# Where ScalarE computes the scan's turns, where GpSimd computes its fractions, and where the new-token bias products stand: one decoder layer step on one Trainium2 core

## The chip, the cores and the metric

The kernel runs on one core of one Trainium2 chip. The metric is the device time of one execution in microseconds (us); lower is better. TensorE is called PE here, VectorE DVE, ScalarE ACT, GpSimd POOL and SyncE SP, as in the profile.

## The reference, cut to what matters

One layer of a hybrid decoder, all in float32, for a prompt of 256 tokens and, in the same pass, for one new token of each of 8 sequences, so that most products have N = 264 columns:

```
z = x @ w_in                                  # q, k, v, u and the two gates, 8192 columns
attn = diff_attention(q, k, v, rel_bias)      # prompt: causal; new tokens: over 16 cached pages of 128 keys each
ssm  = s5_branch(u, ...)                      # 64 groups of complex diagonal states, scanned over the 256 tokens
merged = gate_a * (attn @ w_proj_attn) + gate_s * (ssm @ w_proj_ssm)
h = layer_norm(alpha * x + merged @ w_out)
y = layer_norm(alpha * h + conv_ffn(h, w_up, conv, w_down))
```

The attention adds a bias by distance, `rel_bias[bucket(distance)]`. The kernel makes it as a product of a one-hot table with `rel_bias`: one product for the prompt's distances, two for the cached pages and one of 8 columns for each of the 8 sequences' own new token. The scan rotates by an angle that grows with time. In turns the angle is `time * rate`; its fraction (turns less whole turns) goes into the sine and cosine.

## The kernel before, in words

Weights stream from HBM through a ring of four places of 1 MB (`weight_ring`). Up to about 690 us a column block of `w_in` or `w_glu` is multiplied by `z_group` (line 745, 16 k-tiles of 128x264 float32, each shown in the trace as two records). After that the weights are split into two roundings by ACT (line 1505) and DVE (line 1974), and three products stand for one (lines 1093, 1094 and 1099). The change touches only the part up to 690 us.

Each engine has its own list of instructions, written out by hand, and runs it in that order. Semaphores join them.

- **Setup.** PE multiplies the q blocks. `z_group` takes hooks: a number of a quarter block (four matmuls) after which other work is put in. In the group of q2 and q3, `bias_rows` (lines 777 to 787) stands at hook 3: the products for the prompt's and the pages' biases (lines 779, 781) and then the eight for the new tokens (line 785). ACT copies them out (`setup_copy`, lines 1270 to 1272) ahead of its copy (`evict`) of block q2. The second product's operand is 33 rows by 8 columns.
- **Rounds.** The loop `for i in range(H - 1)` stands in the lists of SP, PE, ACT and DVE. Round i computes head i's prompt attention, the scan of tile t = i + 1 (four steps n = 4t + p), and the cache scores of sequence i + 1, while the cached values of sequence i are multiplied. Between these, PE works off six blocks of `w_in`.
- **The cache.** For every page, SP loads 512 KB of keys and 512 KB of values in a written order ("K9", "V5", ...), in which a key page waits until the page five before it is reduced, and a value page until PE has used the one four before it (`v_used`). POOL multiplies a key page by the query (`products`, line 653, two halves), DVE reduces it (`reduce_page`, line 1807), and PE multiplies the values (`page_pv`, line 725). The values of pages 14 and 15 are loaded and used in the next round ("P14", "P15").
- **The scan.** For a step n, ACT computes `turns(n)` (line 1279), which needs DVE's step n - 2; POOL computes `fractions(n)` (lines 642, 644); ACT the three sine tables in `rotation(n)` (lines 1286 to 1290); DVE `states(t, p)` (lines 1750 to 1763), which sets `xs_ready`. Each table has two places.
- **POOL's order.** In round i, pages 0 to 15 of sequence i + 1, with `fractions` of steps 4i + 6 and 4i + 7 before pages 3 and 5, and of steps 4i + 8 and 4i + 9 before pages 8 and 11.
- **ACT's order in the middle of a round.** `sums_copy(i)`, the copy of the third block, `combined(i - 1)` (the copy of PE's small product at line 914, which stands at hook 15), `final_states(4t + 2)`, `turns(4t + 4)`, the prompt's exponentials, the fourth block.
- **The maxima.** DVE reduces all 16 pages' scores to a maximum (`page_max`, lines 1813 to 1816), starts the next step of the scan, then computes the maximum over partitions (`all_max`, lines 1822 and 1824), on which PE's small product at line 901 waits; the values of pages 14 and 15 follow there at once.

Of the kernel before, what the change touches and what calls it, by code (L numbers as in the profile page):

```python
# [23 lines left out]
B = 8  # L24
N = T + B
H = 8
# [12 lines left out]
HT = SW // P  # L39
NB = 32  # L40
# [122 lines left out]
def build(nc, a, out, scratch):  # L163
    with ExitStack() as ctx:
# [19 lines left out]
        small = sb("small", 592)  # L184
# [124 lines left out]
        def sems(*names):  # L309
            return [sem(n) for n in names]  # L310
# [18 lines left out]
        tr, tr_used = sems("setup_transposed", "setup_copied")  # L329
# [289 lines left out]
        @block.gpsimd  # L619
        def _(pool):  # L620
            ch = Chain(pool, pool_c)
            ch.did(pool.memset(ident[:, :], 0.0))
            ch.wait()
            pool.affine_select(out=ident[:, :], in_=ident[:, :], compare_op=ALU.not_equal, fill=1.0, base=0,
                               pattern=[[-1, P]], channel_multiplier=1).then_inc(const_ready, 1)
            pool.memset(small[0:NB + 1, 32:32 + H], MASK).then_inc(rel_ready, 1)
            for tensor, value in ((ones[:, :], 1.0), (mean_w[:, :], 1.0 / D), (v_mean_w[:, :], 1.0 / P),
                                  (small[:, 4:5], PI / 2), (small[:, 5:6], EPS), (small[:, 6:7], 4 * EPS)):
                pool.memset(tensor, value).then_inc(const_ready, 1)

            times_i = score[0][:, 0:T].bitcast(I32)
            ch.did(pool.iota(times_i, pattern=[[1, T]], base=1, channel_multiplier=0))
            ch.wait()
            pool.tensor_copy(times, times_i).then_inc(times_ready, 1)
            pool.memset(b_pad[:, :], 0.0).then_inc(bpad_zero, 1)
            pool.memset(MT[:, :, 256:512], 0.0).then_inc(mt_zero, 1)

            def fractions(n):

                turns, whole_turns, part = (tab[n % 2][:, k * 256:(k + 1) * 256] for k in range(3))  # L640
                pool.wait_ge(tv_ready, n + 1)
                ch.did(pool.tensor_scalar(whole_turns, turns, 1.5 * 2 ** 23, -1.5 * 2 ** 23, ALU.add, ALU.add))  # L642
                ch.wait()
                pool.tensor_tensor(part, turns, whole_turns, ALU.subtract).then_inc(tf_ready, 1)

            def products(b, p):

                n = PAGES * b + p
                if p == 0:
                    pool.wait_ge(qb_in[b % 2], 16 * (b // 2 + 1))  # L650
                pool.wait_ge(k_in[n % K_PLACES], 16 * (n // K_PLACES + 1))
                for e in range(2):
                    pool.tensor_tensor(half_page(2 * n + e), half_page(2 * n + e), q_b[b % 2][:, e * 512:(e + 1) * 512],  # L653
                                       ALU.mult).then_inc(kq_ready, 1)

            fractions(0)
            fractions(1)
            for p in range(PAGES):
                if p == 1:
                    fractions(2)  # L660
                if p == 3:
                    fractions(3)
                products(0, p)
            fractions(4)
            fractions(5)
            for i in range(H):
                for p in range(PAGES if i + 1 < B else 0):
                    if p == 3:
                        fractions(4 * i + 6)
                    if p == 5:  # L670
                        fractions(4 * i + 7)
                    if p == 8 and i + 2 < HT:
                        fractions(4 * i + 8)
                    if p == 11 and i + 2 < HT:
                        fractions(4 * i + 9)
                    products(i + 1, p)

            def centre(ln):

                pool.wait_ge(mean_copied, ln + 1)  # L680
                for g in (0, 1):
                    c3 = x3[:, 4 * g:4 * g + 4, :]
                    pool.tensor_tensor(c3, c3, mean_y.unsqueeze(1).to_broadcast([P, 4, N]), ALU.subtract  # L683
                                       ).then_inc(cent_ready, 1)

            centre(0)
            centre(1)
# [3 lines left out]
        def _(pe):  # L691
# [42 lines left out]
            def z_group(group, at={}):  # L734

                n, tiles = SLOT[group[0]], y_tiles if group[0][0] == "glu" else x_tiles
                per, step, done = KT // len(group), len(tiles) // 4, 0
                for c in range(len(tiles) // per):
                    g = CHUNK[group[0], c]
                    pe.wait_ge(ring_in[g % SLOTS], 16 * (g // SLOTS + 1))  # L740
                    for m in range(len(group)):
                        if c == 0:
                            wait(pe, z_read, n + m - 1)
                        for k in range(c * per, (c + 1) * per):
                            last = pe.matmul(bank[(n + m) % 2][:, 0:N], chunk_weight(g, k - c * per, m), tiles[k],  # L745
                                             start=(k == 0), stop=(k == len(tiles) - 1))
                            if k == len(tiles) - 1:
                                last.then_inc(slot_done, 1)
                            done += 1
                            if done % step == 0 and done // step in at:  # L750
                                at[done // step]()
# [21 lines left out]
            x_copied(8)  # L773
            z_group((("q", 0), ("q", 1)), {1: lambda: x_columns(2), 2: lambda: x_columns(3), 4: lambda: x_copied(KT)})

            def bias_rows():
                pe.wait_ge(tab_in, 32)
                rel = small[0:NB + 1, 32:32 + H]
                pe.matmul(bank[4][0:H, 0:384], rel, table[:, OH_TOEP:OH_TOEP + 384], start=True, stop=True).then_inc(tr, 1)
                for p in range(2):  # L780
                    last = pe.matmul(bank[5][:, p * H:(p + 1) * H], table[:, OH_PAGE + p * P:OH_PAGE + (p + 1) * P],
                                     rel, start=True, stop=True)
                last.then_inc(tr, 1)
                for b in range(B):
                    last = pe.matmul(bank[6][:, b * H:(b + 1) * H], table[:, OH_NEW + b * P:OH_NEW + (b + 1) * P],
                                     rel, start=True, stop=True)
                last.then_inc(tr, 1)

            z_group((("q", 2), ("q", 3)), {3: bias_rows})

            def first_states():
                pe.wait_ge(tr_used, 3)
# [421 lines left out]
        def _(act):  # L1214
# [119 lines left out]
            def combined(b):  # L1334
                take(("combine", b))
                copy(att3[:, :, T + b].rearrange("p (g e) -> p e g", e=2),
                     bank[2][:, 0:8].rearrange("p (e g) -> p e g", e=2)).then_inc(mail_read, 1)
# [63 lines left out]
            for i in range(H - 1):  # L1401
                t, whole = i + 1, i + 2 < HT
                tiles = [what for group in ROUNDS[i] for what in group]
                if i:
                    attention(i - 1)
                value_rows(i)
                turns(4 * t + 2)
                final_states(4 * t)
                rotation(4 * t + 2)
                if not whole:  # L1410
                    evict(tiles[0])
                turns(4 * t + 3)
                final_states(4 * t + 1)
                if whole:
                    evict(tiles[0])
                sample_exp(i)
                evict(tiles[1])
                if i:
                    copy_sums(i - 1)
                exps(i, 1)  # L1420
                rotation(4 * t + 3)
                if not whole:
                    evict(tiles[2])
                sums_copy(i)
                if whole:
                    evict(tiles[2])
                if i:
                    combined(i - 1)
                final_states(4 * t + 2)
                if t + 1 < HT:  # L1430
                    turns(4 * t + 4)
                exps(i, 0)
                evict(tiles[3])
                final_states(4 * t + 3)
                if t + 1 < HT:
                    turns(4 * t + 5)
                    rotation(4 * t + 4)
                p_diff_copy(i)
                evict(tiles[4])
                if whole:  # L1440
                    rotation(4 * t + 5)
                key_rows(i + 1)
                if whole:
                    evict(tiles[5])
# [740 lines left out]
```

## Time and profile before

| what | value |
|---|---|
| median of 3 runs | 1681.71 us (1678.88 to 1687.78) |
| the profiled execution | 1680.43 us |
| its span in the trace | 1678.6 us |
| PE busy | 1637.3 us, 98% |
| DVE, ACT, POOL busy | 67%, 39%, 23% |
| mean granted TensorE clock | 0.991 |
| HBM traffic | 390.7 MB, 233 GB/s over the span |

The table is to be read as shares of one span. The rows further down give engines their busy time, and in square brackets the idle time before an instruction and what ended it. PE's ends are modelled, so that its busy share says how little it waits, not how near to its peak it is. The profiled execution lies 1.8 us above its span, and 1.3 us below the median.

### The profile page before, as it was taken

The numbers are of one execution on the slowest core, as the hardware profiler recorded it, in microseconds if no ns is written. First come the engines' busy times: TensorE is split into PE (matmuls) and PEld (weight loads), VectorE is DVE, ScalarE is ACT, GpSimd is POOL, SyncE is SP. The second block draws the span as 40 slices with busy tenths as digits, with TensorE's granted clock in tenths as the row PEclk, the third lists the DMA queues.
The fourth block names the chain that finished last, engine by engine and source line by source line (L and its number), as shares of the span: only waits on it lengthen the run. The fifth ranks groups of instructions, "written<-read, shape, count | busy, mean of one in ns | idle before, by whom it ended". The sixth has DMA issues, their size and how long they took to land. (4 is left out here: it accounts for less than half of the span.)

```text
span 1678.6 us, 31242 instructions
## 1 busy us (share of the span) xinstructions
PE 1637.3 (98%) x11730; PEld 1458.6 (87%) x11730; DVE 1123.5 (67%) x1748; ACT 649.8 (39%) x981; POOL 389.2 (23%) x341
## 2 busy tenths in 40 slices
PE   9999999999999999999997999999999999999996
PEld 7878777667766676899996999999999999999995
DVE  2373787887887952876667767777777775545555
ACT  2121344344344313433447444444444443333333
POOL 1066487687687720000001000000000000000001
PEclk9999999999999999999998999999999999999998
DMA  9669799999999988766663676666766666666651
GB/s 252 194 216 346 252 391 376 378 387 377 379 389 372 375 287 264 191 183 180 176 186 97 187 185 176 176 182 180 191 174 177 178 180 172 187 177 181 182 152 53
DMA packets 472151, 391.81 MB, mean 233 GB/s; under 512 B 23550, under 2 KB 436123, under 8 KB 472028
## 3 DMA queue, kind: packets, MB, share of 16 engines
q1 hardware_dynamic: 401388, 323.27, 62.7%
q10 hardware_dynamic: 70656, 67.11, 12.5%
q8 instruction: 67, 1.10, 0.3%
q14 instruction: 40, 0.33, 0.1%
HBM read 385.24 MB, written 5.46 MB: 233 GB/s over the span
## 5 line engine op out<-in xcount | busy, mean ns | idle before, releaser
L745 PE MATMUL bank<-work,weight_ring 128*128 128x264 f32 x2176 | 516.7, 392 | 1.3 <-ACT work L1218 0.7
L1505 ACT ACTIVATE weights_hi<-weight_ring 128x2048 fp32r<-128x2048 f32 (+1 forms) x166 | 309.8, 1866 | 509.6 <-PE bank L1094 386.2
L745 PEld LDWEIGHTS bank<-work,weight_ring 128*128 128x128 f32 x2176 | 405.0, 191 | 88.5 <-issue 21.2
L1974 DVE TENSOR_TENSOR weights_lo<-weight_ring,weights_hi 128x2048 fp32r<-128x2048 f32 (+1 forms) x166 | 369.0, 2224 | 111.4 <-ACT weights_hi L1505 69.9
L1093 PE MATMUL bank<-h_hi,weights_hi 128*128 128x264 f32 x1344 | 331.0, 284 | 0.0
L1094 PE MATMUL bank<-h_lo,weights_hi 128*128 128x264 f32 x1344 | 330.2, 284 | 0.0
L653 POOL TENSOR_TENSOR work<-work 128x512 f32<-128x512 f32 x256 | 318.0, 1277 | 36.8 <-DMA work<-toeplitz_rows 21.2
L1093 PEld LDWEIGHTS bank<-h_hi,weights_hi 128*128 128x128 f32 x1344 | 253.2, 188 | 0.0
L1094 PEld LDWEIGHTS bank<-h_lo,weights_hi 128*128 128x128 f32 x1344 | 252.7, 188 | 0.0
L683 POOL TENSOR_TENSOR work<-work,ffn_scratch 128x1056 f32<-128x1056 f32 x4 | 9.6, 2410 | 1046.7 <-ACT ffn_scratch L1218 1046.7
L1807 DVE TENSOR_REDUCE work<-work 128x8 f32<-128x512 f32 x256 | 165.4, 677 | 64.0 <-POOL work L653 63.5
L1099 PE MATMUL bank<-h_hi,weights_lo 128*128 128x264 f32 x1344 | 176.6, 284 | 0.0
L1093 PE MATMUL bank<-hidden_hi,weights_hi 128*128 128x264 f32 x688 | 169.7, 284 | 1.8 <-DVE ffn_scratch L2104 1.8
L1094 PE MATMUL bank<-hidden_lo,weights_hi 128*128 128x264 f32 x688 | 169.3, 284 | 0.0
L1099 PEld LDWEIGHTS bank<-h_hi,weights_lo 128*128 128x128 f32 x1344 | 168.4, 188 | 0.0
L1218 ACT ACTIVATE work<-bank 128x264 f32<-128x264 f32 (+8 forms) x117 | 40.0, 354 | 278.6 <-PE bank L745 108.0
L1093 PEld LDWEIGHTS bank<-hidden_hi,weights_hi 128*128 128x128 f32 x688 | 129.5, 188 | 2.0 <-DVE ffn_scratch L2104 2.0
L1094 PEld LDWEIGHTS bank<-hidden_lo,weights_hi 128*128 128x128 f32 x688 | 129.4, 188 | 0.0
L2101 DVE SCALAR_TENSOR_TENSOR ffn_scratch<-bank,conv_and_ln_parameters,ffn_scratch 128x255 f32<-128x255 f32 x86 | 41.5, 483 | 125.9 <-ACT ffn_scratch L1218 125.9
L1099 PE MATMUL bank<-hidden_hi,weights_lo 128*128 128x264 f32 x688 | 91.3, 284 | 0.0
L1099 PEld LDWEIGHTS bank<-hidden_hi,weights_lo 128*128 128x128 f32 x688 | 86.7, 188 | 0.0
L642 POOL TENSOR_SCALAR work<-work 128x256 f32<-128x256 f32 x32 | 34.5, 1078 | 183.7 <-ACT work L1279 183.7
(274 smaller groups left out, 1930.6 us busy)
## 6 DMA issues: line engine op xcount, KB each, us to landing
weight_ring<-in_w_up SPq DMA_DIRECT2D x86, 1024.0 KB, 5.6
work<-in_cache_k SPq DMA_DIRECT2D x128, 512.0 KB, 6.8
work<-in_cache_v SPq DMA_DIRECT2D x128, 512.0 KB, 7.1
weight_ring<-in_w_in ACTq DMA_DIRECT2D x60, 1024.0 KB, 13.4
weight_ring<-in_w_down SPq DMA_DIRECT2D x32, 1024.0 KB, 6.0
weight_ring<-in_w_out SPq DMA_DIRECT2D x16, 1024.0 KB, 5.8
weight_ring<-in_w_down SPq DMA_DIRECT2D x16, 704.0 KB, 5.0
weight_ring<-in_w_proj_attn SPq DMA_DIRECT2D x16, 512.0 KB, 4.3
```

The source lines that it names most:

```text
L642: ch.did(pool.tensor_scalar(whole_turns, turns, 1.5 * 2 ** 23, -1.5 * 2 ** 23, ALU.add, ALU.add))
L653: pool.tensor_tensor(half_page(2 * n + e), half_page(2 * n + e), q_b[b % 2][:, e * 512:(e + 1) * 512], ALU.mult).then_inc(kq_ready, 1)
L683: pool.tensor_tensor(c3, c3, mean_y.unsqueeze(1).to_broadcast([P, 4, N]), ALU.subtract).then_inc(cent_ready, 1)
L745: last = pe.matmul(bank[(n + m) % 2][:, 0:N], chunk_weight(g, k - c * per, m), tiles[k], start=(k == 0), stop=(k == len(tiles) - 1))
L1093: pe.matmul(dst[:, 0:N], weight(w_hi, off, k0 + k), highs[k], start=start and k == 0, stop=False)
L1094: last = pe.matmul(dst[:, 0:N], weight(w_hi, off, k0 + k), lows[k], start=False, stop=False)
L1099: last = pe.matmul(dst[:, 0:N], weight(w_lo, off, k0 + k), highs[k], start=False, stop=stop and k == len(highs) - 1)
L1218: return act.activation(dst, src, ACT.Copy, scale=scale)
L1505: act.activation(w_hi[:, (j % 2) * KT * P:(j % 2) * KT * P + k_tiles * P].bitcast(F32R), slot3(j, 0, k_tiles).rearrange("p k m -> p (k m)" ...
L1807: dve.tensor_reduce(score[b % 3][:, p * 16 + 8 * e:p * 16 + 8 * e + 8], half_page(2 * n + e).rearrange("p (m d) -> p m d", d=HD), AX.X, AL ...
L1974: dve.tensor_tensor(w_lo[:, cols].bitcast(F32R), slot3(off % SLOTS, 0, k_tiles).rearrange("p k m -> p (k m)"), w_hi[:, cols], ALU.subtract ...
L2101: n1 = ch.did(dve.scalar_tensor_tensor(y[:, 1:T], ps[:, 0:T - 1], par(1), y[:, 1:T], ALU.mult, ALU.add))
```

## The change

Three things move; nothing is added or left out.

1. In POOL's list, `fractions(4i + 8)` stands before page 11 and not before page 8, and `fractions(4i + 9)` before page 14 and not before page 11 (rounds 0 to 5).
2. In ACT's list, `final_states(4t + 2)` and `turns(4t + 4)` stand ahead of `combined(i - 1)`.
3. The eight bias products for the new tokens leave hook 3 of the group of q2 and q3 and stand in two lots of four, at hooks 5 and 7.

```diff
-                    if p == 8 and i + 2 < HT:
+                    if p == 11 and i + 2 < HT:
                         fractions(4 * i + 8)
-                    if p == 11 and i + 2 < HT:
+                    if p == 14 and i + 2 < HT:
                         fractions(4 * i + 9)
...
-                for b in range(B):
+
+            def new_bias(b0):
+                for b in range(b0, b0 + B // 2):
                     last = pe.matmul(bank[6][:, b * H:(b + 1) * H], table[:, OH_NEW + b * P:OH_NEW + (b + 1) * P],
                                      rel, start=True, stop=True)
-                last.then_inc(tr, 1)
-
-            z_group((("q", 2), ("q", 3)), {3: bias_rows})
+                if b0:
+                    last.then_inc(tr, 1)
+
+            z_group((("q", 2), ("q", 3)), {3: bias_rows, 5: lambda: new_bias(0), 7: lambda: new_bias(B // 2)})
...
-                if i:
-                    combined(i - 1)
                 final_states(4 * t + 2)
                 if t + 1 < HT:
                     turns(4 * t + 4)
+                if i:
+                    combined(i - 1)
                 exps(i, 0)
```

In the lists below a number after x counts what stands together. The first place is PE in the setup, from the end of block q1's work to the first transposes of the next group: line 745 is the block product, 779 and 781 are the biases of the prompt and the pages, and 785 (788 in the changed kernel) the new tokens'. Before:

```order
L745 MATMUL bank<-work,weight_ring 128x264 x36
L779 MATMUL bank<-work,small 8x384
L781 MATMUL bank<-small,work 128x8 x2
L785 MATMUL bank<-small,work 128x8 x8
L745 MATMUL bank<-work,weight_ring 128x264 x24
```

With the change:

```order
L745 MATMUL bank<-work,weight_ring 128x264 x36
L780 MATMUL bank<-work,small 8x384
L782 MATMUL bank<-small,work 128x8 x2
L745 MATMUL bank<-work,weight_ring 128x264 x8
L788 MATMUL bank<-small,work 128x8 x4
L745 MATMUL bank<-work,weight_ring 128x264 x8
L788 MATMUL bank<-small,work 128x8 x4
L745 MATMUL bank<-work,weight_ring 128x264 x8
```

Eleven small products in a row have become three, four and four, with eight block products between them.

The second place is POOL in one round: lines 642 and 644 are one `fractions`, line 653 two halves for each page. The rows begin with `fractions(4i + 7)`. Before:

```order
37 L642 TENSOR_SCALAR work<-work 128x256
38 L644 TENSOR_TENSOR work<-work 128x256
39 L653 TENSOR_TENSOR work<-work 128x512 x6
40 L642 TENSOR_SCALAR work<-work 128x256
41 L644 TENSOR_TENSOR work<-work 128x256
42 L653 TENSOR_TENSOR work<-work 128x512 x6
43 L642 TENSOR_SCALAR work<-work 128x256
44 L644 TENSOR_TENSOR work<-work 128x256
45 L653 TENSOR_TENSOR work<-work 128x512 x16
```

With the change:

```order
37 L642 TENSOR_SCALAR work<-work 128x256
38 L644 TENSOR_TENSOR work<-work 128x256
39 L653 TENSOR_TENSOR work<-work 128x512 x12
40 L642 TENSOR_SCALAR work<-work 128x256
41 L644 TENSOR_TENSOR work<-work 128x256
42 L653 TENSOR_TENSOR work<-work 128x512 x6
43 L642 TENSOR_SCALAR work<-work 128x256
44 L644 TENSOR_TENSOR work<-work 128x256
45 L653 TENSOR_TENSOR work<-work 128x512 x10
```

Six pages (5 to 10) now stand ahead of `fractions(4i + 8)` where three did, and the last lot of pages (14, 15 and the next sequence's 0 to 2) is shorter by three.

The third place is ACT in the middle of a round, from the copy of the sums to the exponentials: 128x2x4 is `combined`, 128x2 `final_states`, line 1279 (1283) `turns`. Before:

```order
L1218 ACTIVATE work<-bank 128x32
L1254 ACT_TABLE_LOAD
L1254 ACTIVATE work<-bank 128x264
L378 DMA weight_ring<-in_w_in 128x8x256
L1218 ACTIVATE work<-bank 128x2x4
L1218 ACTIVATE work<-conv_and_ln_parameters 128x2
L1279 ACTIVATE work<-work,conv_and_ln_parameters 128x256
```

With the change:

```order
L1222 ACTIVATE work<-bank 128x32
L1258 ACT_TABLE_LOAD
L1258 ACTIVATE work<-bank 128x264
L378 DMA weight_ring<-in_w_in 128x8x256
L1222 ACTIVATE work<-conv_and_ln_parameters 128x2
L1283 ACTIVATE work<-work,conv_and_ln_parameters 128x256
L1222 ACTIVATE work<-bank 128x2x4
```

The turns are computed before the copy that waits for PE's hook 15.

## Rows read from the trace of the kernel before

**Rows 1.** The page: span, busy time, and DMA rate in 40 slices of the span.

```profile
PE 1637.3 (98%) x11730; PEld 1458.6 (87%) x11730; DVE 1123.5 (67%) x1748; ACT 649.8 (39%) x981; POOL 389.2 (23%) x341
...
GB/s 252 194 216 346 252 391 376 378 387 377 379 389 372 375 287 264 191 183 180 176 186 97 187 185 176 176 182 180 191 174 177 178 180 172 187 177 181 182 152 53
```

**Rows 2.** PE's timeline, setup: start us, length us, line, xrecords.

```profile
36.84 0.61 PE L781 MATMUL bank<-small,work 33*128 33x8 f32 x4
37.28 2.27 PEld L785 LDWEIGHTS bank<-small,work 33*128 33x128 f32 x16
39.57 13.85 PE L745 MATMUL bank<-work,weight_ring 128*128 128x264 f32 x48
53.04 0.58 PEld L694 LDWEIGHTS bank<-ident,work 128*128 128x128 f32 x4
64.99 10.53 PEld L745 LDWEIGHTS bank<-work,weight_ring 128*128 128x128 f32 x48
75.56 0.58 PEld L694 LDWEIGHTS bank<-ident,work 128*128 128x128 f32 x4
```

**Rows 3.** Stretches: length, busy PE PEld DVE ACT POOL, granted clock, DMA share, GB/s.

```profile
38.00:38.50 0.50, 0.50 (x7) 0.50 (x6) 0.00 (x0) 0.00 (x0) 0.00 (x0) 1.00 1.23 300
38.50:39.00 0.50, 0.50 (x5) 0.50 (x4) 0.00 (x0) 0.00 (x0) 0.00 (x0) 0.65 1.19 291
...
45.00:45.50 0.50, 0.50 (x3) 0.39 (x2) 0.00 (x0) 0.00 (x0) 0.00 (x0) 0.52 2.08 371
```

**Rows 4.** PE's waits in total, 200 to 600 us: us, times, longest.

```profile
PE bank L725 <- DMA work<-in_cache_v: 3.4, 6, 0.8
PE bank L901 <- DVE small L1824: 3.4, 5, 1.2
PE bank L745 <- ACT work L1218: 0.7, 1, 0.7
```

**Rows 5.** POOL's timeline in the round from 367 us.

```profile
396.25 1.07 POOL L642 TENSOR_SCALAR work<-work 128x256 f32<-128x256 f32 x1 [11.09 <-ACT work L1279]
...
407.32 19.95 POOL L653 TENSOR_TENSOR work<-work 128x512 f32<-128x512 f32 x16
```

**Rows 6.** ACT's timeline in the same round.

```profile
392.20 0.39 ACT L1254 ACTIVATE work<-bank 128x264 f32<-128x264 f32 x1 [2.14 <-PE bank L745]
...
395.67 0.50 ACT L1279 ACTIVATE work<-work,conv_and_ln_parameters 128x256 f32<-128x256 f32 x1
...
412.86 0.42 ACT L1286 ACTIVATE work<-work 128x256 f32<-128x256 f32 x1
...
415.75 0.36 ACT L1218 ACTIVATE work<-bank 128x256 f32<-128x256 f32 x1
```

**Rows 7.** DVE's timeline at the end of the round and the start of the next.

```profile
399.40 0.69 DVE L1807 TENSOR_REDUCE work<-work 128x8 f32<-128x512 f32 x1 [5.75 <-POOL work L653]
...
419.73 0.69 DVE L1807 TENSOR_REDUCE work<-work 128x8 f32<-128x512 f32 x1 [0.54 <-POOL work L653]
```

**Rows 8.** PE's timeline, waits at the round starts of 305, 369 and 432 us.

```profile
305.28 0.36 PE L901 MATMUL bank<-small,ones 16*128 16x16 f32 x2 [0.54 <-DVE small L1824]
...
368.91 0.36 PE L901 MATMUL bank<-small,ones 16*128 16x16 f32 x2 [1.24 <-DVE small L1824]
...
431.56 0.36 PE L901 MATMUL bank<-small,ones 16*128 16x16 f32 x2 [0.46 <-DVE small L1824]
433.13 0.62 PE L725 MATMUL bank<-work 128*16 128x256 f32 x8 [0.66 <-DMA work<-in_cache_v]
```

**Rows 9.** SP's page loads in that round: issue time.

```profile
383.35 0.33 SPq L459 DMA_DIRECT2D work<-in_cache_v  x1
...
402.05 0.33 SPq L459 DMA_DIRECT2D work<-in_cache_k  x1
...
422.72 2.59 SPq L459 DMA_DIRECT2D work<-in_cache_v  x3
```

**Rows 10.** DMA, 383 to 433 us: rate, and median us to landing of a key page.

```profile
DMA packets 9442, 19.88 MB, mean 398 GB/s; under 512 B 532, under 2 KB 5910, under 8 KB 9438
...
work<-in_cache_k SPq DMA_DIRECT2D x14, 512.0 KB, 7.4
```

**Rows 11.** PE's timeline: the product that needs the bank which ACT's key rows free.

```profile
418.94 0.70 PE L889 MATMUL bank<-work 128*128 128x256 f32 x2
```

More of the change, by code:

```diff
@@ L774, in _ @@
             z_group((("q", 0), ("q", 1)), {1: lambda: x_columns(2), 2: lambda: x_columns(3), 4: lambda: x_copied(KT)})
+            rel = small[0:NB + 1, 32:32 + H]
             def bias_rows():
                 pe.wait_ge(tab_in, 32)
-                rel = small[0:NB + 1, 32:32 + H]
                 pe.matmul(bank[4][0:H, 0:384], rel, table[:, OH_TOEP:OH_TOEP + 384], start=True, stop=True).then_inc(tr, 1)
```

## The prediction

> **What bounds the kernel now.** I read the page first. PE is busy for 98% of the span and DVE for 67% [rows 1], so the end is set by PE's list; another engine counts only where PE waits for it, or where PE itself runs slower. The 40 slices of the page show a second limit: from about 210 to 590 us the DMA engines move 372 to 391 GB/s, and half of that later. In the rounds PE and the DMA are both close to full.
>
> Second, the granted clock in short stretches, because a PE that is always busy can still be slow. It is full up to 38.5 us, falls inside the stretch from 38.50 to 39.00, and is back at the end of that from 45.00 to 45.50, whose mean is 0.52 [rows 3]; worked out from the means 0.65 and 0.52, it is low from 38.65 to 45.48. PE did not idle before it fell: it ran the small bias products, from 36.84 us on without a stop [rows 2].
>
> Third, PE's waits in the rounds. Six waits for value pages give 3.4 us, five waits of the small product at line 901 for DVE's maximum give 3.4 us, and one wait for an ACT copy gives 0.7 us [rows 4]. That is 7.5 us in 400, and all that the two moves in the rounds can win.
>
> Last, the lists of POOL, ACT and DVE in one round. POOL stands still for 11.09 us ahead of `fractions(4i + 8)`, because ACT writes the turns only at 395.67 [rows 5, 6]. In this time DVE waits 5.75 us for page 8 [rows 7], in the middle of a step of the scan.
>
> **The change part by part.** I count against the profiled execution, 1680.43 us (span 1678.6 us and 1.8 around it), which is 1.3 us below the median of the runs.
>
> *The bias products in two lots.* The work stays the same: eight products, 16 records. What can go is the time at the low clock. The 48 records of the block product after the lot take from 39.57 to 53.04, 13.47 us; the same 48 records at full clock take from 64.99 to 75.56, 10.57 us [rows 2]. That is 2.90 us. The lot itself takes from 37.28 to 39.57, 2.29 us for 16 records; the four records of the same form before it take 36.84 to 37.28, 0.11 us each, so 16 would take 1.76 [rows 2]. That is another 0.5. Half of the time at the low clock, (45.48 - 38.65) / 2 = 3.4, says the same. I take **-3.3 us**: after the change no run of small products is longer than four (0.11 x 8 = 0.9 us) or the prompt's and pages' three, and eight block products (16 records of 0.22, 3.5 us) stand between them, so the clock should have no reason to fall. The bounds are 0 (it falls all the same) and -3.4. All of it lies on PE, which nothing else holds up there.
>
> Here a rule speaks against the edit. The trace shows the clock falling with PE busy in every stretch [rows 3]. The Trainium skill, page "TensorE: Matmul & The Clock Gate", section "Part 1: The HAM clock gate", gives the low level as the state after an idle window. By that rule, small products are not idleness, splitting them would win nothing, and this term would be 0. I go by the row, in which nothing but the small products stands ahead of the fall. The same section says that the window runs freely and does not restart with the kernel, which no row of one execution can show; by it the fall need not come in every execution of the kernel before, and the term would be smaller in a median.
>
> ACT's copies behind the lots are costed at nothing. The new tokens' biases are complete two lots of eight block products (3.5 us each) and two of four small ones (0.9 us each) after 37.3, at 46.1 us; ACT's copy of q2 stands behind that. PE next needs q2's bank at the group's end, four block products (1.8 us) later, and two ACT copies take 0.6 us (a block copy is 0.39 [rows 6]). If that cover were gone, PE would lose under 1 us once.
>
> *POOL's fractions three pages later.* POOL no longer stands still for 11.09 us: pages 5 to 10 run on at 2.5 us each (19.95 us for eight [rows 5]). What it gains is not all handed on, because page 11 and those behind it are loaded late anyway. A key page needs its fifth predecessor reduced and its turn in SP's list, where the value pages wait for PE. So DVE's last reduction, at 419.73 now [rows 7], moves by something between 0 and the 5.75 us by which page 8 is free sooner; I take the middle, 3 us, since half of SP's list are value pages that wait for PE. The maximum moves by 3 us too. The waits at line 901, at most 1.24 us [rows 8], would go.
>
> *Turns ahead of the combination.* The turns move from 395.67 to just behind the third block's copy, 392.20 + 0.39 = 392.6 [rows 6], 3 us sooner. POOL now asks for them after page 10, at about 393 at the earliest, so that both moves fit together. Behind the turns `combined` still waits for PE, and is 0.6 us later at most by the two moved instructions; PE next needs its bank at hook 21, over 10 us later. Cost nothing.
>
> *What PE gets of it.* Of the five waits at line 901, two (0.54 and 0.46, [rows 8]) stand directly ahead of a wait for a value page. The page comes when it comes, so the 1.0 us saved there is lost again. The other three give 3.4 - 1.0 = 2.4 us. The 0.7 us for the ACT copy [rows 4] depends on the first step of the scan in the round, which starts sooner too. I take **-3.1 us** for both moves. The bounds are -7.5 (all waits of [rows 4]) and, below nothing, the fourth rival.
>
> Why the value pages don't come sooner: the value page that SP issues at 383.35 waits for PE; from there to 433 us the DMA runs at a mean of 398 GB/s [rows 9, 10]. Pages 14 and 15 of the values are issued from 422.72 on and the second is in time for 433.13 [rows 8, 9]. Issuing them 3 us sooner puts them into the same full queue.
>
> Sum: 1680.43 - 3.3 - 3.1 = **1674.0 us**, 0.5% under the median. A measurement of this kernel can tell about 0.5%, 8.4 us from the median, so 1673.3 is the border of faster.
>
> **The rivals.**
>
> *The DMA sets the pace (slightly faster, 1677.1).* If each round is as long as its loads need at 398 GB/s, every wait at line 901 turns into one for a value page, and only the clock's 3.3 us are left: 1680.43 - 3.3 = 1677.1. For it speak the rate [rows 10] and the waits for pages [rows 4]; against it, that three of five waits at 901 have no page wait behind them. The Trainium skill, page "DMA: Bandwidth & Descriptors", section "Issuing engines are not separate DMA queues", says that all loads run on the same 16 engines, whoever issues them: by that rule too, an earlier issue buys no bandwidth.
>
> *All waits go (1669.6).* The key loads spread into the time in which POOL stood still, the queue is shorter when the value pages come, and all 7.5 us go: 1680.43 - 3.3 - 7.5. For it: SP stops for key pages that POOL holds up, page 13 being issued only at 402.05, after the late reduction of page 8 [rows 7, 9].
>
> *The clock falls anyway (1677.3).* Then the change does not do what its third part is meant to do: the biases' other three products still stand together, and the lots of four are small too. 1680.43 - 3.1 = 1677.3. Against it: the clock stood until 38.5, though small products had run since 36.84 [rows 2, 3], and no lot will be that long.
>
> *ACT stands in front of POOL (slower, 1692).* `fractions(4i + 9)` now come after page 13, and ACT's `rotation(4i + 9)`, at 412.86 [rows 6], stands ahead of its copy of the key rows (415.75, done 416.1), whose bank PE needs at 418.94 [rows 6, 11]. The slack is 2.8 us. Page 13 is issued at 402.05 and lands after a median of 7.4 us, at 409.5 [rows 9, 10]; its product (2.5) and the fractions (1.8) end at 413.8, 0.9 us after ACT asks, inside the slack. Only if page 13 lands 1.9 us later than that does PE lose, one for one, in each of six rounds. With 2.5 us beyond this point: 6 x 2.5 = 15, and 1680.43 - 3.3 + 15 = 1692. Against it: the page should be issued sooner, not later, than now.
>
> **How the numbers follow.** The forecast (1672.5 to 1675.5) has a chance of 0.33, all waits go 0.25, the DMA sets the pace 0.28, the clock falls anyway 0.08, ACT in front of POOL 0.06. The runs of the kernel before spread by 9 us around the median, so the range is the cases from 1669.6 to 1677.3, widened by 2.6 us below and, as the median of before may lie 1.3 us and more above its profile, by 4.7 above: 1667 to 1682 leaves out most of the fourth rival and little else. Faster by over 0.5%: all of "all waits go" and a third of the forecast and a bit, 0.38. Slower: 0.06. Within: 0.56.
>
> **What the profile after would show.** The granted clock at 1.0 in every stretch from 36 to 50 us, and 48 block records in about 10.6 us. POOL's waits for turns shorter by about 11 us a round, DVE's 5.75 us wait for page 8 gone, line 901 without waits, the waits for value pages no longer in sum than 3.4 us plus one. The forecast is wrong if the clock still falls near 40 us, if the waits for value pages grow by what line 901 loses, or if PE waits for an ACT copy at line 889.

## The result, and the profile after

The changed kernel takes 1670.49 us (median of 15 runs, 1669.02 to 1678.26) against 1685.93 us (15 runs, 1678.3 to 1690.62) for the kernel before, measured with it. The ratio is 0.9923, 95% interval 0.9908 to 0.9938: faster by 0.8%. The forecast was 1674.0, range 1667 to 1682; the time lies next to that of the rival "all waits go" (1669.6), which had 0.25. The profiled execution took 1671.36 us, 9.07 less than the one before.

First PE's waits between 200 and 560 us, in total; they answer to [rows 4]:

```profile
PE bank L725 <- DMA work<-in_cache_v: 0.2, 1, 0.2
```

This is the only line left. In it, after the colon, stand the total in us, the number of waits and the longest. The five waits at line 901 (905 now) and five of the six for value pages are gone.

PE's timeline in the setup answers to [rows 2]:

```profile
35.20 0.81 PE L780 MATMUL bank<-work,small 33*8 33x384 f32 x2
...
40.24 1.05 PE L788 MATMUL bank<-small,work 33*128 33x8 f32 x8
41.22 3.83 PE L745 MATMUL bank<-work,weight_ring 128*128 128x264 f32 x16
44.98 1.06 PE L788 MATMUL bank<-small,work 33*128 33x8 f32 x8
...
49.63 0.60 PE L694 MATMUL bank<-ident,work 128*128 128x128 f32 x4
```

The same two places in the profile before:

```profile
36.10 0.81 PE L779 MATMUL bank<-work,small 33*8 33x384 f32 x2
...
53.26 0.60 PE L694 MATMUL bank<-ident,work 128*128 128x128 f32 x4
```

The clock does not fall. From the first small product to the transposes it takes 14.43 us (35.20 to 49.63), where it took 17.16 (36.10 to 53.26), and PE reaches the transposes 3.6 us sooner than before; 0.9 of this was won before the first small product (35.20; 36.10 before), in PE's start, which the change doesn't touch.

POOL's timeline in the same round (from 359 us here) answers to [rows 5]:

```profile
369.01 7.42 POOL L653 TENSOR_TENSOR work<-work 128x512 f32<-128x512 f32 x6
377.21 2.49 POOL L653 TENSOR_TENSOR work<-work 128x512 f32<-128x512 f32 x2 [0.77 <-DMA work<-in_cache_k]
385.60 2.49 POOL L653 TENSOR_TENSOR work<-work 128x512 f32<-128x512 f32 x2 [5.90 <-DMA work<-in_cache_k]
389.46 2.50 POOL L653 TENSOR_TENSOR work<-work 128x512 f32<-128x512 f32 x2 [1.38 <-DMA work<-in_cache_k]
391.93 1.07 POOL L642 TENSOR_SCALAR work<-work 128x256 f32<-128x256 f32 x1
```

The 11.09 us ahead of the fractions are gone; POOL now waits for key pages instead, up to 5.90 us. Its waits in sum, 200 to 560 us (before: 92.6 us for the turns, 0.8 for key pages):

```profile
POOL work L653 <- DMA work<-in_cache_k: 57.3, 37, 5.9
POOL work L642 <- ACT work L1283: 25.7, 12, 3.1
```

ACT writes the turns at 387.13, 4.8 us ahead of their use, and `rotation(4i + 9)` and the copy of the key rows stand where they stood, 3.2 us ahead of PE's product at line 893 (889 before):

```profile
387.13 0.51 ACT L1283 ACTIVATE work<-work,conv_and_ln_parameters 128x256 f32<-128x256 f32 x1
...
409.49 0.36 ACT L1222 ACTIVATE work<-bank 128x256 f32<-128x256 f32 x1
```

```profile
410.98 1.14 PE L841 MATMUL bank<-work 32*128 32x256 f32 x8
...
412.67 0.70 PE L893 MATMUL bank<-work 128*128 128x256 f32 x2
```

What had not been read closely is the DMA's rate inside a round. Of the 180 stretches of 2 us from 200 to 560 us, 12 are below 300 GB/s in the kernel before, in one cluster in each round. These are the ones of the round from 367 us (busy PE, PEld, DVE, ACT, POOL, clock, DMA share, GB/s), before:

```profile
372.00:374.00 2.00, 2.00 (x11) 1.71 (x10) 1.97 (x4) 0.58 (x2) 2.00 (x3) 1.00 1.04 397
374.00:376.00 2.00, 2.00 (x13) 1.37 (x13) 1.97 (x4) 0.69 (x3) 0.59 (x2) 1.00 0.91 299
376.00:378.00 2.00, 2.00 (x17) 1.13 (x14) 1.97 (x5) 1.99 (x4) 1.92 (x3) 1.00 1.00 385
378.00:380.00 2.00, 2.00 (x10) 1.71 (x10) 2.00 (x5) 1.98 (x8) 2.00 (x2) 1.00 0.83 174
380.00:382.00 2.00, 2.00 (x14) 1.37 (x16) 1.90 (x4) 1.96 (x4) 2.00 (x3) 1.00 0.95 254
```

And the same part of the round after, some 6 us sooner in the span, in stretches of 4 us (in stretches of 2 us none of this part is below 373 GB/s):

```profile
366.00:370.00 4.00, 4.00 (x19) 3.23 (x17) 3.97 (x8) 2.60 (x5) 2.74 (x3) 1.00 1.04 399
370.00:374.00 4.00, 4.00 (x25) 2.69 (x25) 2.64 (x5) 2.81 (x8) 4.00 (x5) 1.00 1.05 392
374.00:378.00 4.00, 4.00 (x31) 2.62 (x30) 3.93 (x7) 1.76 (x4) 3.23 (x3) 1.00 1.04 388
```

In each round before there was a moment in which too few page loads were queued (the thin moment, from here on); now 4 such stretches are left in the 180, in two rounds. The 16 DMA engines were not idle in it: their busy share is 0.83 to 0.95 in the three rows under 300 GB/s. In the two lowest, what was left to them was mostly small packets (255 of 282, and 506 of 506, under 2 KB), above all those of the next sequence's query (512 KB, `load_query`). The packets from 380 to 382 us before, and from 370 to 372 us after, where the query is loaded too but beside pages:

```profile
DMA packets 506, 0.51 MB, mean 254 GB/s; under 512 B 9, under 2 KB 506, under 8 KB 506
...
DMA packets 420, 0.79 MB, mean 396 GB/s; under 512 B 13, under 2 KB 298, under 8 KB 420
```

Who held the page loads up is told by SP's waits at line 458, from 200 to 600 us, first before and then after:

```profile
SPq L458 <- DVE work L1807: 104.1, 72, 3.8
SPq L458 <- PE bank L725: 58.7, 31, 4.9
...
SPq L458 <- PE bank L725: 111.6, 46, 5.9
SPq L458 <- DVE work L1811: 49.1, 49, 2.6
```

SP waited for DVE to reduce a key page, which waits for POOL, for 104.1 us; now for 49.1. It now stands mostly where a value page's place is still in use, that is, ahead of PE. In the 16 us that end with the thin moment (366 to 382 us before) it waited 5.6 us for reductions. The stand of POOL that comes before this moment is that of the round before: it ended at 333.61, and from there to 364.6 POOL worked without a pause and waited for no page, so that SP had to wait for it; the stand of this round begins at 385.16, after the moment.

The mean over 200 to 560 us rose from 382 to 391 GB/s. This proves nothing by itself, because the same loads are now done in less time.

Where the 9.07 us of the two profiles lie: 3.6 up to the transposes, 7.7 more by the value pages' product of the last round (572.71 before, 561.36 after), and then 2.3 are lost again, of which 1.7 by a new fall of the clock for 3.4 us at about 586 us and 0.6 by a longer wait of PE at line 972 (1.32; 0.72 at line 968 before).

### The profile page after: what moved, and what is told of

It reads as the page before. It is cut to its first block and busy times, and to the rows that moved or that the text cites. A ratio compares the mean times of both kernels' runs of the same rounds, so it can differ in the third digit from the quotient of the medians.

```text
span 1669.6 us, 31242 instructions
## 1 busy us (share of the span) xinstructions
PE 1634.0 (98%) x11730; PEld 1457.5 (87%) x11730; DVE 1125.2 (67%) x1748; ACT 650.6 (39%) x981; POOL 390.4 (23%) x341
## 5 line engine op out<-in xcount | busy, mean ns | idle before, releaser
L725 PE MATMUL bank<-work 128*16 128x256 f32 x1024 | 68.6, 383 | 0.9 <-ACT work L1222 0.6
```

Source lines behind the costliest of these rows:

```text
L725: last = pe.matmul(bank[5][32 * g:32 * g + 16, 0:2 * P], score[b % 3][:, p * 16:(p + 1) * 16], page(v_pages, n)[:, g * 2 * P:(g + 1) * 2 * ...
```

## The experiments

Two theories at the start. **A**, for the setup: the unbroken row of small products lowers the clock. **B**, for the rounds: the key pages that POOL held up stopped SP's list, and with it the value pages. The rival to B was the forecast's own step, a full queue in which value pages come when they come.

Each run's ratio is to the kernel before, as measured beside it. The waits are those of one profile of each kernel.

**The parts alone.** The bias products alone (the third part of the change):

> Only the new tokens' bias products in two lots; rounds as before. Theory A (the unbroken row of small products lowers the clock): no stretch below full clock near 40 us, 2.7 to 3.3 us less than before, PE's waits in the rounds as before (line 901 3.4 us, value pages 3.4 us). Rival (the fall has another cause and its absence in the one trace was luck): a fall of 6.8 us near 40 us, time as before. Ratio by theory A 0.998.

Measured: 1680.18 us (12 runs), ratio 0.9987, 0.9966 to 1.0008. No fall near 40 us. PE's waits from 200 to 600 us:

```profile
PE bank L725 <- DMA work<-in_cache_v: 6.8, 9, 1.2
PE bank L905 <- DVE small L1828: 1.7, 2, 1.2
```

The interval holds the 2.7 to 3.3 us that were expected (0.9984 to 0.9980), and it holds no gain at all. The waits at 905 have halved against [rows 4] and those for value pages have doubled though nothing in the rounds was changed; their sum rose from 6.8 to 8.5 us. So they differ this much from one execution to the next, and a value page can be waited for in place of line 901, as the forecast had it.

Both moves in the rounds, the bias products as before:

> Both moves in the rounds, bias products as before. Theory B (key pages that POOL held up stopped SP's list, and the value pages behind them): waits of PE at line 901 and for value pages near 0, POOL waits for key pages about 58 us, first transposes after the setup products at 53 us as before, 7.5 us less than before. Rival (the DMA queue is full, value pages come when they come; the one trace was luck): line 901 near 0 but value pages 3.4 us or more, 2.4 us less. Ratio by theory B 0.9955, by the rival 0.9985.

Measured: 1671.42 us (6 runs), ratio 0.9920, 0.9892 to 0.9949; value waits 0.2 us, none at line 901, POOL waits 57.2 us for key pages. That is the whole gain of the change, and more than the 7.5 us that were expected (0.9955, outside the interval). But the clock did not fall in this trace either, although the eleven small products stand in one row:

```profile
35.88 0.81 PE L779 MATMUL bank<-work,small 33*8 33x384 f32 x2
36.62 0.61 PE L781 MATMUL bank<-small,work 33*128 33x8 f32 x4
37.09 1.93 PE L785 MATMUL bank<-small,work 33*128 33x8 f32 x16
38.94 10.95 PE L745 MATMUL bank<-work,weight_ring 128*128 128x264 f32 x48
49.73 0.60 PE L694 MATMUL bank<-ident,work 128*128 128x128 f32 x4
```

From line 779 to the transposes: 13.85 us here, without a fall and without a split; 17.16 in the profile before (36.10 to 53.26), with a fall; 14.43 after. So a fall costs 3.3 us, as estimated, the split costs 0.6 us, and the fall comes in some executions only: with the products in one row it is in 2 of the 7 profiles (the kernel before, the first of the turns alone), with the change's two lots in none of 4. In the two with a fall line 779 starts at 36.10 us, in the other five at 35.24 to 35.88. If a fall had the same chance of 2 in 7 with the lots, four profiles without one would still come in a quarter of such cases, so these four do not show that the lots prevent it.

POOL's two fractions alone (first part of the change):

> Only POOL's two fractions three pages later; ACT's turns still behind the combination. POOL reaches them near 393 us in the frame of before and the turns stand at 395.7, so POOL waits 1 to 3 us a round for the turns of step 4i + 8 where it waited 11 to 12. Theory B: this part carries nearly all of the rounds' gain: PE's waits at line 901 and for value pages under 1 us together, 6 to 7.5 us less. Rival (both moves are needed): half of the waits stay.

Measured: 1671.03 us (6 runs), ratio 0.9925, 0.9896 to 0.9953; no wait of PE at 901 or for value pages, POOL waits at most 0.35 us for the turns of 4i + 8 (1 to 3 were expected) where it waited 11 to 12. As expected by B, the part carries all of the gain; again the gain is more than the waits explain (6 to 7.5 us would be 0.9955 and above).

ACT's turns alone (second part of the change):

> Only ACT's turns ahead of the combination; POOL's fractions still before pages 8 and 11. POOL's wait for the turns falls by 3 us a round, from 11 or 12 to 8 or 9. Theory B: page 8 is reduced 3 us sooner, but POOL still waits for the turns of step 4i + 9 or is held less, and about half of PE's 6.7 us of waits in the rounds goes, 2 to 4 us less. Rival: nothing, since the later fractions set the last page: within 1 us of before.

Measured: 1672.07 us (12 runs, 1668.08 to 1684.67), ratio 0.9938, 0.9913 to 0.9963. This is more than either theory had allowed. Seven of the runs lie from 1668 to 1672.4 us and five from 1676 to 1684.7; the profiled one was the slowest, 1684.67 us. The second profile:

> The same kernel as the turns alone, for a second profile: seven of its twelve runs lay at 1668 to 1672 us, the profiled one at 1684. If the queue running dry sets the time, a run near 1670 has few stretches under 300 GB/s, though POOL still waits 8 to 10 us a round for the turns; if it has as many as before (12), that account of the gain is wrong or incomplete.

Measured: 1669.51 us, with 3 stretches under 300 GB/s. POOL's waits in it:

```profile
POOL work L642 <- ACT work L1279: 86.3, 19, 10.0
POOL work L653 <- DMA work<-in_cache_k: 0.5, 1, 0.5
```

POOL still waits 86.3 us in sum where it waited 92.6 (9.3 to 10.0 ahead of `fractions(4i + 8)` where it was 11.1 to 12.3), and up to 560 us PE has no wait at 901 or for a value page. In this execution, two microseconds less of standing still in a round were enough. In the first profile of the same kernel the last round's start has it otherwise (4 us stretches, columns as above):

```profile
550.00:554.00 4.00, 2.64 (x12) 1.80 (x12) 3.86 (x8) 0.00 (x0) 0.20 (x1) 1.00 1.04 411
554.00:558.00 4.00, 2.02 (x9) 1.40 (x8) 3.93 (x8) 0.08 (x1) 0.00 (x0) 1.00 0.29 87
```

PE stands still for 2.6 and 3.7 us there (up to 551.36 and 559.75), waiting for DVE's maximum, and the DMA is nearly idle while it does. The trace shows what was late, POOL's row of products (timeline, 500 to 562 us) and DVE's addition of the bias to the scores (line 1813, the first step of the maximum):

```profile
530.52 19.68 POOL L653 TENSOR_TENSOR work<-work 128x512 f32<-128x512 f32 x16
543.60 6.88 DVE L1813 TENSOR_TENSOR work<-work 128x256 f32<-128x256 f32 x1
```

The addition takes 0.42 us where POOL is idle as it starts, and 0.75 to 1.53 where it starts inside one of POOL's products; then it ends 0.3 us after that product. Here it ended 0.3 us after the whole row (550.20). Of 112 such additions in the 14 profiles of this document one more did so, for 4.43 us (values first, at 226.17). Why in these two and not in the others was not found. Of the 15.2 us between the two profiles of the turns alone, 9.2 are waits of PE (2.6 and 3.7 for the maximum, 2.9 for value pages), 3.6 lie ahead of the transposes, where the clock fell in the first, and about 1.7 are a second fall, from 560 us on.

One line of POOL's list alone:

```diff
-                    if p == 8 and i + 2 < HT:
+                    if p == 11 and i + 2 < HT:
                         fractions(4 * i + 8)
```

> The kernel before with one line changed: fractions of step 4i + 8 before page 11 (as in the change), those of 4i + 9 left before page 11 too, so both stand together. Turns behind the combination. The theory by now (POOL's long stand ahead of page 8 lets the DMA queue run dry once a round): the 11 to 12 us waits go, no more than 4 stretches of 2 us under 300 GB/s between 200 and 560 us, PE's waits for line 901 and value pages under 1 us, the gain of POOL's part in full (ratio 0.992). If POOL now waits several us for the turns of 4i + 9 before page 11, half of the gain: ratio 0.996.

Measured: 1672.72 us (10 runs), ratio 0.9938, 0.9912 to 0.9965; the profile shows no wait of PE at 901 or for value pages and 4 stretches under 300 GB/s; POOL waits 0.9 us at most for the turns of 4i + 9. The first fraction is what counts.

**Value pages first.** SP's order alone, in the kernel before:

```diff
-("Sk", "P14", "P15", "V0", ...
+("Sk", "V0", ...
-"N0", "N1", "V13", "N2", "N3", "N4"
+"N0", "N1", "V13", "V14", "V15", "N2", "N3", "N4"
...
```

> The kernel before, with SP alone changed: the values of pages 14 and 15 are loaded at the end of their own round, ahead of the next key pages 2 to 4, and not behind them in the next round. POOL, ACT and PE as before. Theory B (the value pages were late because SP stood at key pages that POOL held up): the waits for value pages 14 and 15 directly behind line 901 vanish, line 901's waits stay (3 to 5 us), the waits in mid-round for page 7 stay; 1 to 2 us less. Rival (a full DMA queue sets their landing, whenever issued): value waits stay at 3 us or more, time within 1 us of before.

Measured: 1681.25 us (12 runs), ratio 0.9982, 0.9952 to 1.0011. The waits for pages 14 and 15 vanished as B said, but the sum, 7.5 us, did not go:

```profile
PE bank L721 <- DMA work<-in_cache_v: 5.0, 5, 1.3
PE bank L897 <- DVE small L1820: 2.5, 3, 1.3
```

The value waits now stand in the middle of the rounds (1.31, 1.23 and 1.10 us). B in its narrow form falls: the place of the two pages in SP's list is not the cause. Twelve stretches under 300 GB/s are still there, and SP still waits 90.1 us for reductions. This gave the theory held since: as long as the queue runs out of page loads once a round, the loads lost there are missing later, wherever PE next needs a page.

The same order in the changed kernel:

> The changed kernel with SP's order of the run before this one. The waits of PE in the rounds are 0.2 us there, so nothing is left to win: within 0.1% of the changed kernel (about 1670.5), if the key pages 2 to 4, now behind two value pages, aren't late for POOL. If they are, POOL's round starts later, line 901 waits again, and it is 1 to 3 us slower.

Measured: 1669.75 us (8 runs), ratio to before 0.9921, 0.9893 to 0.9950: as the changed kernel, with 4 such stretches.

The profiles side by side, 200 to 560 us, by SP's waits for DVE's reductions of key pages, 2 us stretches below 300 GB/s, and PE's waits at 901 and for value pages:

| kernel | SP's waits, us | stretches | PE's waits, us |
|---|---|---|---|
| before | 99.0 | 12 | 6.8 |
| bias products alone | 93.7 | 11 | 8.5 |
| values first | 90.1 | 12 | 7.5 |
| turns alone, first profile | 69.6 | 7 | 6.6 |
| turns alone, second profile | 73.7 | 3 | 0 |
| POOL alone | 39.6 | 3 | 0 |
| first fraction alone | 40.5 | 4 | 0 |
| both moves | 41.8 | 1 | 0.2 |
| changed kernel | 49.1 | 4 | 0.2 |

The columns go together in eight of the nine. The ninth, the first profile of the turns alone, is no witness: 3.7 of its 6.6 us and two of its seven stretches are the addition of 6.88 us and what followed from it. In the values first, 1.35 of the 7.5 us come behind the addition of 4.43 us. That the thin moment causes the waits is argued from the order in time (in the profile before it ends 17 us and more before a page is missing), not shown by a run that changes the rate alone.

**The clock by itself.** The eight new tokens' products done four times over, 32 small products in one row:

```diff
-            z_group(..., {3: bias_rows, 5: lambda: new_bias(0), 7: lambda: new_bias(B // 2)})
+            z_group(..., {3: bias_rows, 6: lambda: new_bias(0, 4).then_inc(tr, 1)})
```

> The changed kernel with the new tokens' bias products done four times over, 32 in one row at hook 6 (same outputs). Theory A: PE runs small products for 7 us without a stop (24 more of 0.22 us, 5.3 us of work) and the clock falls in this row in any execution, for 6.8 us or more; the setup up to the first transposes is 5.3 us of work and 3 to 5 us of clock longer than in the changed kernel. Rival (small products count as activity, only idleness lowers the clock): no fall, 5.3 us longer.

Measured: 1680.08 us (one run). The stretches around the row, which runs from 43.64 to 52.50:

```profile
46.00:48.00 2.00, 2.00 (x20) 2.00 (x20) 0.00 (x0) 0.00 (x0) 0.00 (x0) 1.00 0.43 78
48.00:50.00 2.00, 2.00 (x16) 2.00 (x15) 0.00 (x0) 0.00 (x0) 0.00 (x0) 0.76 0.54 134
50.00:52.00 2.00, 2.00 (x11) 2.00 (x11) 0.00 (x0) 0.00 (x0) 0.00 (x0) 0.50 0.02 6
```

PE is busy throughout by the profile, in which its ends are modelled: it waits for nothing. The clock falls. The same 32 in four lots of eight, at hooks 4 to 7:

> The same 32 small products in four lots of eight at hooks 4 to 7, with four block products (1.8 us) between lots. Theory A, if the length of a row decides: no fall, 5.3 us longer than the changed kernel up to the first transposes, 3 to 5 us less than the row of 32. If the share of small products in a few microseconds decides, as half of this stretch is small products, the clock falls here too.

Measured: 1674.83 us (one run), no fall:

```profile
40.00:44.00 4.00, 4.00 (x27) 3.44 (x26) 0.00 (x0) 0.00 (x0) 0.00 (x0) 1.00 0.41 81
44.00:48.00 4.00, 4.00 (x27) 3.44 (x27) 0.00 (x0) 0.00 (x0) 0.00 (x0) 1.00 0.49 108
48.00:52.00 4.00, 4.00 (x27) 3.44 (x27) 0.00 (x0) 0.00 (x0) 0.00 (x0) 1.00 0.20 33
```

From the first small product to the transposes it is 20.37 us (36.73 to 57.10) against 22.76 (36.82 to 59.58) in one row, 2.4 us less for the same work. Theory A holds in one profile each. A fall would be missing by chance in all six profiles with lots (the four above, this one and the next) in about one of eight cases, again at 2 in 7, so the series leans to A and does not settle it.

The changed kernel with one lot of eight at hook 5 in place of two of four:

> The changed kernel with the eight new tokens' products in one lot at hook 5 and the three others at hook 3. The lots of eight with block products between them had no fall of the clock, so none here either: 48 block records near 40 us at full clock, time within 3 us of the changed kernel.

Measured: 1671.91 us (one run), no fall, 14.14 us from line 780 to the transposes (35.41 to 49.55), 0.3 less than with two lots.

**A wait that was left.** In the last round, DVE's sum on which PE waits, ahead of page 11's reduction (with the values first):

```diff
-                reduce_page(b, 11)
+                if i != H - 2:
+                    reduce_page(b, 11)
                 if i == H - 2:
                     dve.wait_ge(bs_done, HT // 2)
...
+                    reduce_page(b, 11)
```

> The changed kernel with the values of pages 14 and 15 loaded in their own round, and in the last round DVE's sum for the new tokens' states (on which PE's product at line 972 waits 1.3 us) ahead of page 11's reduction. That wait falls below 0.3 us and nothing else changes: 1 us less than the changed kernel, about 1669, which the interval may not show. Rival: POOL or the maximum is late instead, no gain.

Measured: 1669.14 us (7 runs), ratio to before 0.9923, 0.9895 to 0.9951. The wait is gone from the profile (1665.2 us of span), but the interval cannot tell this version from the changed kernel, so nothing is claimed for it.

## Why the prediction was right or wrong

*What bounds the kernel:* right for the profiled execution, in which PE's waits in the rounds were 7.5 us and went. The runs gained more (below).

*The bias products, -3.3 us:* the price of one fall was right, 3.3 us measured (17.16 - 13.85). The size of the term is too large for a median. I set it against one execution, in which the clock fell; 5 of 7 profiles with the products in one row have no fall, and the split, costed at nothing, takes 0.6 us. An estimate from these few profiles, if the lots do prevent the fall, is 3.3 x 2/7 - 0.6 = 0.3 us in the mean. The runs can't tell this from 3.3: alone the part measured 0.9987, and its interval holds both. The rule that the window runs freely (the Trainium skill, "TensorE: Matmul & The Clock Gate", "Part 1: The HAM clock gate") had been cited for just this and left out of the sum; the traces agree with it. The rule of the same section by which the low level follows on idleness would have given no term. The row of 32 shows a fall while PE waits for nothing, so that in this case a fall does not need a pause in PE's list; whether the array is idle inside such small products the modelled ends can't show.

*POOL's fractions:* right in kind. DVE's last reduction moved from 419.73 to 411.23, and PE's round start from 417.24 to 410.98; against that start it came 2.2 us sooner (forecast 3). The waits at line 901 went.

*The turns ahead of the combination:* 3 us sooner, at no cost, right. That both moves fit together was right but beside the point: either one alone gives 0.9925 or 0.9938, both give 0.9920, with intervals that overlap. They don't add up.

*What PE gets of it, -3.1 us:* this step failed. It said that a value page "comes when it comes" and that issuing sooner "puts them into the same full queue". The DMA was at its full rate from 383 to 433 us, the stretch that was read, but not from 374 to 382. With the thin moment filled, value pages come in time and 7.3 of the 7.5 us of waits went (7.7 by the two profiles). The hand-over from line 901 to the value pages, on which 1.0 us rested, is seen only in kernels with twelve or so thin stretches (bias products alone, values first). The Trainium skill ("DMA: Bandwidth & Descriptors", "Issuing engines are not separate DMA queues") has all loads on the same 16 engines, from which I had drawn that an earlier issue buys no bandwidth. No run speaks against the page; what I drew from it holds only while page loads are always queued, and the stretches at 174 to 299 GB/s, with SP waiting for reductions ahead of them, show that they were not.

*The rivals:* "all waits go" came true, and the reason given for it, SP stopped by key pages that POOL holds up, fits SP's waits. That its time of 1669.6 was met so closely is in part luck, since it counts 3.3 us for a fall that most executions don't have. "The clock falls anyway" did not come in any profile with the lots. "The DMA sets the pace" fell with the step above. ACT in front of POOL did not come: the copy of the key rows stands 3.2 us ahead of PE's product, as it did.

The chances leaned to "within 0.5%"; measured was faster by 0.8%. That 1670.49 lies in the range is owed to the rival, which the range had been drawn to hold, and not to the forecast's own mechanism; its two terms erred in opposite ways, one too large and one too small.

*What the sum does not cover:* the gain of the runs, 13 us by the ratio, is more than the 9.07 of the two profiles and than the 7.3 of waits. Part of the distance is the yardstick: the kernel before measured 1685.93 in these runs and 1681.71 in the three that were shown, and its profiled execution was among the better ones. Its runs spread over 12 us, those of the changed kernel over 3 us but for one, and no profile of one of its worse executions was kept. A candidate is the addition of line 1813: both long ones, of 6.88 and 4.43 us, are in kernels in which POOL still stands ahead of page 8 and then works a long row without a pause (5 profiles), none in the 9 with the first fraction moved. This is not shown to be the cause; it stays open.

## What to carry to other kernels

Where a transfer queue looks full, read its rate in stretches much shorter than a round, and with it what the packets are and what the issuing engine waits for: the waits that follow from one thin moment a round come later, and move about when only the order of the loads is changed. The engine whose waiting holds the loads up can be one with a busy share of 23%. Where a gain in the runs is larger than what two profiles explain, take a profile of a worse execution before the sum is called complete. A gain seen in the granted clock of one execution is to be checked in several, because the same instructions keep the clock in one execution and lose it in the next.

## What the runs showed of the hardware

- PE without a pause on products of 33 rows by 8 columns lost its clock: for 6.8 us in the row of 32 (from 49.0 to 55.9 us), with the row running 43.64 to 52.50. Eight such products in 1.9 us between block products of 2.0 us kept it.
- The eleven in a row (35.88 to 38.94 where the clock held) lost it in 2 of 7 profiles, each time from about 38.65 to 45.5 us.
- Each lot of small products put between block products costs about 0.3 us of PE beside its own work: 13.85 us from the first small product to the transposes with no lot apart, 14.14 with one lot of eight, 14.43 with two of four.
- The DMA engines with a busy share of 0.95 on packets under 2 KB alone moved 254 GB/s; with pages beside them, at a share of 1.03, 396 GB/s.
- DVE's addition of 128x256 took 0.42 us beside an idle POOL, 0.75 to 1.53 when it started inside a product of POOL, and in 2 of 112 cases it lasted until POOL's whole row had ended (4.43 and 6.88 us).
